# Modulation products in column strips, scores by halves, and the first recurrence's outputs placed by ScalarE

## The reference, cut to what matters

```
mod = einsum('bd,de->be', silu(c), w_ada) + b_ada      # 9 rows of c, 6 x 1024 columns
h = x * (1 + sc1) + sh1                                # sh1, sc1 are the first two parts of mod
z = einsum('bld,de->ble', h, w_in)                     # q, k, v, gates
# per head, per chunk of tokens (b: running sum of the log decays inside the chunk):
scores[i, j] = sum_k q[i,k] k[j,k] exp(b[i,k] - b[j,k])   for j <= i
o = scores @ v + (q * exp(b)) @ s
s = s * exp(b_last) + (k * exp(b_last - b))^T @ v
oa = rmsnorm(oa, w) * silu(ga)
...
```

## Time and profile before

| | us |
|---|---|
| median of three runs | 2076.36 |
| profiled execution, own time | 2077.7 |
| its span, first to last instruction | 2075.9 |
| TensorE busy (95% of the span) | 1972.5 |
| VectorE busy (34%) | 696.5 |
| ScalarE busy (21%) | 445.5 |
| GpSimd busy (20%) | 420.5 |

### The profile page before, as it was taken

One profiled execution on the slowest core, in us unless ns is written; L12 is line 12 of the kernel. 1 busy time (PEld: TensorE's weight loads), 2 busy tenths in 40 slices (PEclk: granted clock), 3 DMA queues, 4 the chain that ended last, 5 costly groups with the idle time before them and its releaser, 6 DMA issues.

```text
span 2075.9 us, 24423 instructions
## 1 busy us (share of the span) xinstructions
PE 1972.5 (95%) x7628; PEld 1224.6 (59%) x7628; DVE 696.5 (34%) x1473; ACT 445.5 (21%) x946; POOL 420.5 (20%) x661
## 2 busy tenths in 40 slices
PE   6999999999999999999969999999999999999994
PEld 1754548587858757888857444444444444444443
DVE  1113980499049943000147411111111111111114
ACT  1203431344134443000021111111111111111111
POOL 0001430144014300000000612222222222222220
PEclk9899999999999989999978899999999999999997
DMA  9112432200220083311021599999999999999962
GB/s 387 41 41 85 161 127 84 81 27 19 83 81 2 4 325 123 145 59 41 9 80 62 203 388 372 362 374 364 375 362 372 358 373 368 364 372 360 377 178 93
DMA packets 56941, 419.50 MB, mean 202 GB/s; under 512 B 6289, under 2 KB 10001, under 8 KB 31145
## 3 DMA queue, kind: packets, MB, share of 16 engines
q1 hardware_dynamic: 33689, 339.44, 40.8%
q0 software_dynamic: 21456, 78.10, 14.5%
q10 hardware_dynamic: 1728, 1.05, 0.2%
HBM read 362.96 MB, written 55.61 MB: 202 GB/s over the span
## 4 chain that ended last, share of the span: by engine, by line
PE 83%; DVE 9%; ACT 3%; issue 2%; POOL 1%; DMA 1%; SPq 0%; POOLq 0%; DVEq 0%; ACTq 0%
PE ps L1023 24%; PE ps L1045 12%; PE ps L885 11%; PE ps L846 8%; PE ps L831 7%; PE ps L1014 3%; PE ps L917 3%; PE ps L776 2%; DVE work L1419 2%; PE ps L466 2%; DVE Xb L1426 1%; PE ps L802 1%; PE ps L984 1%; ACT work L572 1%; ACT work L570 1%
## 5 line engine op out<-in xcount | busy, mean ns | idle before, releaser
L1023 PE MATMUL ps<-W,work 128*128 128x512 f32 x1168 | 515.8, 595 | 1.5 <-ACT work L1206 1.2
L1023 PEld LDWEIGHTS ps<-W,work 128*128 128x128 f32 x1168 | 217.1, 191 | 247.9 <-issue 247.9
L1045 PE MATMUL ps<-work 128*128 128x512 f32 x576 | 259.1, 592 | 0.0
L1725 DVE SCALAR_TENSOR_TENSOR work<-ps,work 128x256 f32<-128x256 f32 x73 | 35.3, 484 | 514.5 <-ACT work L1212 514.5
L846 PE MATMUL ps<-Hb,W 128*128 128x260 f32 x768 | 173.4, 389 | 0.0
L1045 PEld LDWEIGHTS ps<-work 128*128 128x128 f32 x576 | 103.8, 190 | 103.3 <-issue 103.3
L846 PEld LDWEIGHTS ps<-Hb,W 128*128 128x128 f32 x768 | 148.7, 194 | 24.3 <-ACT work L1106 0.7
L1241 POOL TENSOR_TENSOR work<-work 128x128 f32<-128x128 f32 x168 | 83.0, 527 | 388.1 <-ACT work L572 388.1
L1735 DVE COPY work<-ps 128x512 f32<-128x512 f32 x144 | 99.6, 692 | 179.3 <-DMA ffrows<-work 92.5
L1311 POOL DMA_INDIRECT ffrows<-work x72 | 115.7, 1607 | 192.2 <-DVE work L1735 121.6
L831 PE MATMUL ps<-W,Hb 128*128 128x512 f32 (+1 forms) x320 | 138.4, 592 | 0.0
(11 more groups left out here) (250 smaller groups left out, 2177.0 us busy)
## 6 DMA issues: line engine op xcount, KB each, us to landing
W<-wexp SPq DMA_DIRECT2D x74, 2048.0 KB, 8.8
work<-wexp SPq DMA_DIRECT2D x73, 1024.0 KB, 8.0
W<-wq SPq DMA_DIRECT2D x36, 2048.0 KB, 8.2
work<-st_in SPq DMA_DIRECT2D x8, 1024.0 KB, 8.1
st_out<-work SPq DMA_DIRECT2D x8, 1024.0 KB, 7.3
Xb<-xT SPq DMA_DIRECT2D x2, 2080.0 KB, 17.3
h2rows<-work SPq DMA_DIRECT2D x5, 512.0 KB, 2.6
yT<-Xb SPq DMA_DIRECT2D x2, 1040.0 KB, 5.3
```

Of the source, the lines that this page charges most:

```text
L1023: mm = pe.matmul(ps[:, k % 2, :], xe[:, k % 2, c, :], GU[:, k % 4, c, :], start=(c == 0), stop=(c == KC - 1))
L1045: mm = pe.matmul(ps[:, 4 + hf, :], aT[:, k % 2, f, :], WD[:, k, f, hf * 512:(hf + 1) * 512], start=(f == 0), stop=(f == 1))
```

## The change

Four edits, all in float32 as before. (1) silu(c) is written into a zeroed buffer of 32 columns per block (`cond32`); the eight products of a modulation quad go to four strips of 32 partitions, two into each strip. `copy_rows` copies all 128 partitions, and `mod_turn` multiplies them with a 0/1 table `fold` that turns the rows and adds the strips in one product. (2) Scores: level 0 is one product of the first 64 keys with the second 64 queries; levels 1 to 6 and the diagonal are two products of 64 x 64 each, for the two halves of the chunk. Scores of even and odd steps have a PSUM bank each, so that the wait is for the mask two steps back. (3) `mask` multiplies 64 x 7 columns in 128 partitions, copies level 0 (64 x 64) into `ST`, and adds up the seven levels in two reductions over 64 partitions each; one quarter of `ST` stays zero. (4) take_o of the first recurrence moves from VectorE to ScalarE, to the front of step c.

```
-                    mm = pe.matmul(ps[0:NCOND, mod_bank(n), :], conds[:, c, :], ring[:, q % 4, :, c, :],
-                                   start=(c == 0), stop=(c == KC - 1))
+                    strip = slice(32 * (c % 4), 32 * (c % 4) + 32)
+                    mm = pe.matmul(ps[strip, mod_bank(n), :], cond32[:, c, :], ring[:, q % 4, :, c, :],
+                                   start=(c < 4), stop=(c >= 4))
...
-                    mm = pe.transpose(ps[:, 5, at:at + NCOND], mod_rows(n)[:, u * P:(u + 1) * P], ident[0:NCOND, 0:NCOND])
+                    mm = pe.matmul(ps[:, 5, at:at + NCOND], mod_rows(n)[:, u * P:(u + 1) * P], C("fold"), start=True, stop=True)
...
-                since(pe, s_pm, n)
-                for l in range(LEV):
-                    pe.matmul(ps[:, l // 4, (l % 4) * CH:(l % 4 + 1) * CH], M[:, p, l, col_], M[:, p, l, col_],
-                              start=True, stop=True)
-                pe.matmul(ps[:, 1, 3 * CH:4 * CH], M[:, p, 9, col_], q4[:, h, cc * CH:(cc + 1) * CH],
-                          start=True, stop=True).then_inc(s_sc, 1)
+                since(pe, s_pm, n - 1)
+                out = levels[n % 2]
+                first, second = (slice(c * CH + r.start, c * CH + r.stop) for r in blocks)
+                pe.matmul(out[blocks[0], :, 7], M[:, p, 0, first], M[:, p, 0, second], start=True, stop=True)
+                for l in range(1, LEV):
+                    for r, at in zip(blocks, (first, second)):
+                        pe.matmul(out[r, :, l - 1], M[:, p, l, at], M[:, p, l, at], start=True, stop=True)
+                for r, at in zip(blocks, (first, second)):
+                    mm = pe.matmul(out[r, :, 6], M[:, p, 9, at], q4[:, h, cc * CH + r.start:cc * CH + r.stop],
+                                   start=True, stop=True)
+                mm.then_inc(s_sc, 1)
...
+            def take_o(n):
+                h, cc = n // 4 % 4, n % 4
+                act.wait_ge(s_ot, n + 1)
+                o = ps[:, 6, 0:v].rearrange("p (j t) -> p j t", t=CH)
+                for j in range(2):
+                    ins = act.activation(oa[:, 2 * h + j, cc * CH:(cc + 1) * CH], o[:, j, :], ACT.Copy, scale=halfw[:, j:j + 1])
+                ins.then_inc(s_oc, 1)
...
             for c in range(17):
                 even = c % 2 == 0 and 2 <= c <= 12
+                if gi == 0 and c >= 2:
+                    take_o(c - 2)
                 if gi == 0 and c % 2 == 0 and c:
                     copy_rows(3 + c // 2)
...
-                    dve.tensor_tensor(Pm, ps[:, 0:2, :].rearrange("p b t -> p (b t)"), C("masks"), ALU.mult).then_inc(s_pm, 1)
+                    dve.tensor_tensor(Pm, levels[n % 2][:, :, 0:7], C("masks").rearrange("p (t l) -> p t l", l=8)[:, :, 0:7],
+                                      ALU.mult)
+                    since(dve, s_o, n - 1)
+                    dve.tensor_copy(ST[blocks[0], n % 2, blocks[1]], levels[n % 2][blocks[0], :, 7]).then_inc(s_pm, 1)
                     dve.wait_ge(s_pm, n + 1)
-                    since(dve, s_o, n - 1)
-                    dve.tensor_reduce(ST[:, n % 2, :], Pm.rearrange("p (l t) -> p t l", l=8), AX, ALU.add).then_inc(s_st, 1)
+                    for r in blocks:
+                        ins = dve.tensor_reduce(ST[r, n % 2, r], Pm[r], AX, ALU.add)
+                    ins.then_inc(s_st, 1)
```

More of the change, by code:

```diff
@@ L36 @@
 LEV = 7
+BL = CH // 2
 GH, GV = 4, 256
@@ L80 @@
                          ("wgk1", KC * RANK)])
-CONST, NCONST = columns([("ident", P), ("ones", P), ("mean", P), ("masks", 8 * P), ("reset", NT), ("mhalf", 1), ("eps", 1)])
+CONST, NCONST = columns([("ident", P), ("ones", P), ("mean", P), ("masks", 8 * BL), ("reset", NT), ("mhalf", 1), ("eps", 1),
+                         ("fold", NCOND)])
 ROUTE, NROUTE = columns([("tri", P), ("iota", P), ("group", NG), ("quads", MAXT // 4), ("part", 1),
@@ L96, in constants @@
     masks = []
-    for l in range(LEV):
+    jb, ib = j % BL, np.arange(BL)[None, :]
+    for l in range(1, LEV):
         s = CH >> (l + 1)
-        masks.append((j // (2 * s) == i // (2 * s)) & (j % (2 * s) < s) & (i % (2 * s) >= s))
-    masks.append(j == i)
-    put(CONST, c, "masks", np.stack(masks, 1).reshape(P, 8 * P))
+        masks.append((jb // (2 * s) == ib // (2 * s)) & (jb % (2 * s) < s) & (ib % (2 * s) >= s))
+    masks += [jb == ib, np.zeros((P, BL))]
+    put(CONST, c, "masks", np.stack(masks, 2).reshape(P, 8 * BL))
     t = np.arange(NT)
@@ L104, in constants @@
     put(CONST, c, "mhalf", -0.5)
+    put(CONST, c, "fold", (j % 32 == np.arange(NCOND)[None, :]))
     put(CONST, c, "eps", EPS)
@@ L177, in decoder_step @@
         qrows = view(Xb, 1088, 12 * DEC * 32, "p (h n) -> p h n", h=12)
-        Pm = view(Xb, 2336, 1024)
+        Pm = view(Xb, 2336, 7 * BL, "p (t l) -> p t l", l=7)
+        blocks = [slice(0, BL), slice(BL, CH)]
+        levels = [ps[:, b, :].rearrange("p (t l) -> p t l", l=8) for b in range(2)]
         ST = view(Xb, 3360, 256, "p (b t) -> p b t", b=2)
@@ L414, in mod_rows @@
         def mod_rows(n):
-            return view(work, 512 * n, 512)[0:NCOND, :] if n < 4 else side[0:NCOND, 0:512]
+            return view(work, 512 * n, 512) if n < 4 else side[:, 0:512]
         def mod_bank(n):
@@ L635, in recurrence_act @@
             store_state(4 * gi + 3)
+            if gi == 0:
+                take_o(15)
         def layer_norm_dve(dve, which):
@@ L1074, in _ @@
             act.wait_ge(s_small, 48)
[L1075 removed]
+            act.wait_ge(s_cs, 1)
+            act.activation(cond32[:, :, 0:NCOND], conds, ACT.Silu).then_inc(s_cs, 1)
             def copy_rows(n):
@@ L1353, in _ @@
             dve.tensor_tensor(H[:, :, SEQ:NT], H[:, :, SEQ:NT], md[:, SH1:SH1 + 8, 1:NCOND], ALU.add).then_inc(s_h, 1)
+            dve.wait_ge(s_h, 9)
+            dve.memset(ST[blocks[1], :, blocks[0]], 0.0).then_inc(s_zst, 1)
             for gi in range(3):
@@ L1451, in take_o @@
                     o = ps[:, 6, 0:v].rearrange("p (j t) -> p j t", t=CH)
[L1452 to L1456, removed]
+                    if gi == 1:
                         dve.tensor_scalar(dst, o, halfw[:, 2:3], None, ALU.mult).then_inc(s_oc, 1)
@@ L1467, in _ @@
                 for c in range(18):
-                    if c >= 2:
+                    if gi and c >= 2:
                         take_o(base + c - 2)
```

10 lines of the change are left out of this document (7 added, 3 removed).

## The result

The changed kernel takes 2038.56 us (median, 2036.94 to 2039.29) against 2075.93 for the kernel before on the same chip: ratio 0.9821, interval 0.9807 to 0.9836. 2041 was predicted, from 2024 to 2062. The profiled execution has a span of 2035.1 us (own time 2036.94), against 2075.9.

The account below looks back on a forecast made before the run. TensorE bounds the start; in the recurrences TensorE and VectorE are nearly full and the chain of waits decides. Gains 11.5 + 6 + 10 + 8 = 35.5 us take 2077.7 to 2042.2, as median 2041 us, range 2024 to 2062.

Parts of the forecast that it names:

- S: Length of a chunk's scores on TensorE: by halves 1.35 us instead of 2.1, bounds 1.05 and 3.9.
- Start: 11.5: Kernel start, modulation in four strips: H starts at 30.2 to 33.7 us instead of 43.61, 11.5 us gained.
- x at 30.2: Kernel start: the load of x lands at 30.2 us, with shorter constants worth 0.6 us.
- C: Rival, scores of all 48 chunks: halves don't overlap, scores cost up to 3.9 us, whole 2130 us; chance 0.05.
- Mask: 2.0: Mask on VectorE, per chunk: falls from 3.08 to 2.0 us, or 2.5 at the old reduction rate.
- First recurrence: 6: First recurrence, all edits: 10.2 us gained at full clock, less 4 charged for pairs at 1.2 GHz, leaving 6.
- The loop at full clock: First recurrence, chain of one pair of chunks from decays to decays: 14.85 us, 0.6 under 15.44.
- Second: 10: Second recurrence: pairs fall from 14.83 to 13.52 us; with 4.8 at the ends 11.3, of which 10 taken.
- Third: 8: Third recurrence: 8 us gained, as the root (L1247, up to 2072 ns) stays slow where it meets VectorE's diffs.
- rival B: Second and third recurrence: root stuck behind diffs in every pair, pairs 14.85, 11.5 us lost, whole 2053; chance 0.12.
- A: Rival: TensorE at lower clock throughout the first recurrence, pairs 18.4 us, stage 10 longer, whole 2057; chance 0.15.
- D: Rival: strips don't overlap at 512 columns, start and fills unchanged, some 15 of 35.5 us lost, 2056; chance 0.03.

## Why the prediction held, point by point

**What bounds, and the new chain: right.** In the first recurrence mk, scores, output, L494 (now L508), ScalarE's take_o, square; in the other two decays, mq, mask, gate value, diffs. The three conditions named for being wrong: S is 1.07, the first recurrence lies within the 113 us from 183 to 296, but H did wait for a load, until 33.7 (34 was the mark).

**Start: 11.5, measured 9.9**, the lower end of its range. TensorE's side came out: modulation is done at 31.67, so without a wait for x H would have come some 11.9 earlier. The term that failed is x at 30.2: it landed at 33.66, and the block ahead of it at 27.16 instead of 25.4, so the last parts had nothing of the 0.6 that the shorter constants were to bring. ("What follows waits for no load" was said of the projections behind H, and holds: 149.8 against 149.7.) The range's upper end, 33.7, is not the sum of its terms either: with one slow turn they make 32.2, with two 34.3. A block cost 1.92 at full clock, where 1.75 was expected, and up to 3.5 where TensorE had waited for the block before.

**S: 1.35, measured 1.07**, the lower bound 1.05. The halves lie wholly beside each other. So C falls. The Trainium skill's rule that a change of tiling mode drains the array ("TensorEngine Tiling (Array Packing)", "Key Properties") leaves nothing to see here: 30 records between products of full width take 1.07.

**Mask: 2.0, measured 1.96** (438.50 to 440.46 in the chain above).

**First recurrence: 6, measured 10.2.** The clock was charged at 4; the five pairs lie 4.4 above five of 13.95, so the charge was right. The loop at full clock was put at 14.85 and is 13.95. The missing 0.9: S 0.28, kd's turning 0.28 (the scores begin before it has ended), the turn 0.15, the square 0.11, take_o and copy_rows 0.15, against 0.07 that mk and the output took more. Nearly all of these terms I had read from pieces in order of time, where an instruction's duration overlaps the next one's; the chain shows only what each adds. That the pairs average 14.84, just what the loop was put at, is luck: they are 13.95 and 0.89 of lower clock, which the prediction charged on top. In its own terms the four pairs from the second decays on gained 2.9, where 2.4 less 4 was written down, the first chunks 5.6 against 4, and the last ones 1.8 against 3.8. Of the four edits, the two that the prediction gave most words to in this stage, strips and take_o, brought nothing there together: strips took 3.0 off "first" and take_o, ahead of the square, put 2.8 back.

**Second: 10, measured 7.3.** Pairs are 13.84, not 13.52: decays 0.11, mq to gate value 0.18 and diffs 0.04 longer. The ends gave 2.5 of the 4.8. At the last chunks ScalarE's copy of kd waits, TensorE idles, and the next gate fill takes 5.20 where the one after it takes 3.51, which is 1.7 of the missing 2.3:

```profile
475.84 0.27 ACT Xb L613
...
476.64 5.20 PE ps L830 x16
...
484.00 3.51 PE ps L830 x16
```

**Third: 8, measured 11.3.** I let the root stay stuck behind diffs ("that stays"); it doesn't: L1276 never takes more than 443 ns, against 2072. Before, three roots begin early in diffs, last until diffs end and stand in the chain with 2.08 us; after, the chain goes from diffs straight to decays, and a root that meets diffs begins in their last instructions. Three pairs were 15.29 long, the other two 14.2; after, all five are 13.2 to 13.3, so the mis-sized term is worth 3.3. So rival B falls the other way round. The Trainium skill's rule on VectorE's and GpSimd's lock ("SBUF — State Buffer", "SBUF: two separate sides") has no long root left to explain in this kernel.

**Rivals.** A came half true: granted clock 0.89 and four of five pairs wholly or partly at the lower clock, but worth 4.4 us and not 16. D falls: a block takes 1.92 us. The sum, 35.5, against 40.8 of span and 37.4 of medians, is near by luck: the terms missed on both sides (1.6 and 2.7 too much, 4.2 and 3.3 too little).

## What to carry to other kernels

An instruction moved off a nearly full engine helps only if that engine ends the wait: ask what stands behind it in the queue it moves to, and put it into a spell where that queue waits anyway. Making one engine faster makes it idle, and TensorE then pays with its clock on the links that do count; unused products in the idle spell gave 1.7 to 6.5 us back in "first". Before adding durations into a chain, subtract their overlaps, best by taking each piece from the chain of waits.

## What the hardware showed that I had not expected

- Sixteen records of 80 columns (2.0 us) in an idle spell of 2.5 us lifted the granted clock of 183 to 280 us to 1.00, against 0.87 with the same order and without them.
- Two column halves run in parallel, by the times of their records: 30 records of 64 columns in 1.07 us, 36 ns each, against 131 ns for one of 128 columns in the earlier trace rows (half of that, halved again by running side by side, would be 33).
- VectorE's reduction costs 1.37 ns for each of 448 columns side by side (614 ns), against 1.9 for each of 1024 with a stride.
- A block of program fetched by DMA (16,384 bytes, 1.08 us) lands among the loads; x's last part came 6.5 instead of 5.0 us behind the block before it, which fits the one meeting the other.
